# MoE layer of a hybrid block: when ScalarE copies gate outputs and gathered tokens, and behind which up tile TensorE folds the gate

## The reference

```python
def swiglu(h, wg, wu, wd):
    a = jnp.einsum('bsd,df->bsf', h, wg)
    b = jnp.einsum('bsd,df->bsf', h, wu)
    return jnp.einsum('bsf,fd->bsd', jax.nn.silu(a) * b, wd)

def moe_swiglu(h, router_w, wg, wu, wd):
    logits = jnp.einsum('bsd,de->bse', h, router_w).astype(jnp.float32)
    top_val, top_idx = lax.top_k(logits, TOP_K)
    gates = jax.nn.softmax(top_val, axis=-1)
    ...
    for e in range(N_EXPERTS):
        out = out + combine[..., e:e + 1].astype(h.dtype) * swiglu(h, wg[e], wu[e], wd[e])
```

## Time and profile before

| | us |
|---|---|
| median of 3 runs | 1413.13 |
| lowest and highest run | 1411.94, 1414.52 |
| profiled execution, its own time | 1415.2 |
| profiled execution, span of the core | 1413.4 |

### The profile page before, as it was taken

How to read it: one execution, slowest core, us unless ns; L and a number is a source line. 1 busy time by engine, 2 the same in 40 slices (tenths; PEclk the granted TensorE clock), 3 DMA queues, 4 the chain that set the end, 5 groups by cost and what they waited for, 6 DMA issues and landing times.

```text
span 1413.4 us, 17326 instructions
## 1 busy us (share of the span) xinstructions
PE 1364.1 (97%) x6732; PEld 1116.9 (79%) x6733; DVE 1143.1 (81%) x794; ACT 1001.7 (71%) x745; POOL 82.3 (6%) x72
## 2 busy tenths in 40 slices
PE   9999999999999999999999999999999999989996
PEld 7997788888799877877777878778777777767785
DVE  5886444544677688999989999988999997989997
ACT  6465434334556578788888888888888888878885
POOL 1011000000000021002000003000005000300000
PEclk9999999999999999999999999999999999999999
DMA  9637555655465349999999999999999999999993
GB/s 346 230 107 246 186 179 187 198 182 164 126 214 164 112 153 347 410 406 413 405 409 381 413 413 408 406 405 366 410 414 412 407 406 397 401 413 414 408 397 159
DMA packets 129530, 445.54 MB, mean 315 GB/s; under 512 B 9696, under 2 KB 13984, under 8 KB 114992
## 3 DMA queue, kind: packets, MB, share of 16 engines
q1 hardware_dynamic: 124912, 433.92, 80.5%
q0 software_dynamic: 2592, 7.45, 1.5%
q10 hardware_dynamic: 1952, 3.18, 0.6%
HBM read 437.70 MB, written 6.82 MB: 315 GB/s over the span
## 4 chain that ended last, share of the span: by engine, by line
PE 67%; DVE 14%; DMA 7%; issue 6%; ACT 5%; ACTq 0%; SPq 0%; DVEq 0%
PE ps L1588 18%; PE ps L1590 18%; PE ps L1589 18%; DVE w_lo L1407 10%; DMA raw<-in_moe_w_down_dram 4%; ACT w_hi L769 3%; DMA raw<-in_moe_w_gate_dram 2%; PE ps L1852 2%; PE ps L1854 2%; PE ps L1874 1%; DVE w_lo L1009 1%; PE ps L1880 1%; DMA raw<-in_moe_w_up_dram 1%; PE ps L1936 1%; ACT fold L818 1%
## 5 line engine op out<-in xcount | busy, mean ns | idle before, releaser
L1407 DVE TENSOR_TENSOR w_lo<-raw,w_hi 128x2048 fp32r<-128x2048 f32 x333 | 749.6, 2288 | 66.9 <-ACT w_hi L769 64.6
L769 ACT ACTIVATE w_hi<-raw 128x2048 fp32r<-128x2048 f32 x332 | 630.8, 1916 | 132.8 <-PE ps L1590 75.9
L1009 DVE TENSOR_TENSOR w_lo<-raw,w_hi 128x2048 fp32r<-128x2048 f32 (+2 forms) x81 | 176.8, 2186 | 98.6 <-ACT w_hi L587 98.3
L587 ACT ACTIVATE w_hi<-raw 128x2048 fp32r<-128x2048 f32 (+2 forms) x81 | 148.2, 1831 | 102.4 <-PE ps L1590 101.5
L1852 PE MATMUL ps<-w_hi,aG 128*128 128x512 f32 x448 | 183.9, 410 | 12.5 <-DVE w_lo L1407 11.7
L1854 PE MATMUL ps<-w_lo,aG 128*128 128x512 f32 x448 | 177.5, 396 | 0.0
L1588 PE MATMUL ps<-w_hi,aG 128*128 128x512 f32 x448 | 175.1, 391 | 2.4 <-DVE w_lo L1407 2.4
L1590 PE MATMUL ps<-w_hi,aG 128*128 128x512 f32 x448 | 174.5, 389 | 0.0
L1589 PE MATMUL ps<-w_lo,aG 128*128 128x512 f32 x448 | 174.4, 389 | 0.0
L1588 PE MATMUL ps<-w_hi,aT_hi 128*128 128x512 f32 (+2 forms) x432 | 161.0, 373 | 4.4 <-DVE aT_lo L1028 2.6
L1590 PE MATMUL ps<-w_hi,aT_lo 128*128 128x512 f32 (+2 forms) x432 | 158.2, 366 | 0.0
(11 more groups left out here) (341 smaller groups left out, 1762.0 us busy)
## 6 DMA issues: line engine op xcount, KB each, us to landing
raw<-in_moe_w_gate_dram SPq DMA_DIRECT2D x112, 1024.0 KB, 9.4
raw<-in_moe_w_up_dram SPq DMA_DIRECT2D x112, 1024.0 KB, 9.7
raw<-in_moe_w_down_dram SPq DMA_DIRECT2D x112, 1024.0 KB, 9.4
raw<-in_w_in_dram SPq DMA_DIRECT2D x20, 1024.0 KB, 6.9
raw<-in_ffn_w_gate_dram SPq DMA_DIRECT2D x14, 1024.0 KB, 5.1
raw<-in_ffn_w_up_dram SPq DMA_DIRECT2D x14, 1024.0 KB, 5.1
raw<-in_ffn_w_down_dram SPq DMA_DIRECT2D x14, 1024.0 KB, 5.0
raw<-in_w_out_dram SPq DMA_DIRECT2D x8, 1024.0 KB, 5.1
```

The source lines that it names most:

```text
L587: nc.scalar.activation(w_hi[:, slot % SPL, 0:n], raw[:, slot, 0:n], ACT.Copy).then_inc(hi_ready, 1)
L769: nc.scalar.activation(moe_hi(pos), raw[:, slot, :], ACT.Copy).then_inc(hi_ready, 1)
L1009: V.tensor_tensor(w_lo[:, slot % SPL, 0:n], raw[:, slot, 0:n], w_hi[:, slot % SPL, 0:n].bitcast(F32), ALU.subtract).then_inc(lo_ready[slot ...
L1407: V.tensor_tensor(moe_lo(pos), raw[:, pos % 6, :], moe_hi(pos).bitcast(F32), ALU.subtract)\
```

## The change

Three things move; no instruction is added or taken away.

1. On ScalarE `copy_g(7)` stands ahead of the split of tile 80 instead of behind it. This is so in all four pairs.
2. Where a next pair follows (three times), the copies of gather fills 0 and 1 stand ahead of `silu_b(7)` and `copy_u(7)` instead of behind them.
3. On TensorE the gate fold of the wide side-B units (1, 3 and 5) stands behind the second up tile instead of the first. In unit 7 it stays behind the first. This is twelve places in the four pairs.

```diff
@@ -851,14 +851,15 @@
                 silu(6, u0, g0)
                 splits(73, 77)
                 evac_sT(6, u0)
-                splits(78, 80)
+                splits(78, 79)
                 copy_g(7)
-                splits(81, 82)
+                splits(80, 82)
+                if more:
+                    gather_pair(p, 0)
+                    gather_pair(p, 1)
                 silu_b(7)
                 copy_u(7)
                 if more:
-                    gather_pair(p, 0)
-                    gather_pair(p, 1)
                     splits(83, 83)
                     gather_pair(p, 2)
                     gather_pair(p, 3)
@@ -1917,7 +1918,7 @@
                     pe.wait_ge(m_sT_lo, u0 + i)
                     for t in range(tiles):
                         proj(i, U_AT[i] + t, 2, t)
-                        if is_b(i) and t == 0:
+                        if is_b(i) and t == (1 if wide(i) else 0):
                             pe.wait_ge(g_copied, b0 + (i + 1) // 2)
                             fold_in(0, 0, 2 if wide(i) else 1, g_folded)
```

## The result

The changed kernel took 1415.86 us, the median of 20 runs, against 1413.53 us for 20 runs of the kernel before. The ratio is 1.0015, with a 95% interval of 1.0008 to 1.0022: slower, by 1.1 to 3.1 us, where 0.2 us less was forecast. The profiled execution took 1415.27 us, its span is 1413.4 us, and its mean granted clock is 0.992, against 1415.2, 1413.4 and 0.994 before.

The account below looks back on a forecast made before the run. The prediction took the weight stream to bound the kernel, each pair lasting as long as its loads. Clock 0.1 and last pair 0.1, all else 0, took 0.2 us off 1413.13, giving 1412.9 us, range 1410.2 to 1415.4.

Parts of the forecast that it names:

- used up, to within 0.1 us: Unit 3 of the first pair: the late gate fold ends at 616.1 to 616.2, SiLU starts at 616.11, leaving no slack.
- the named reason: Between pairs: gather copy 2 stays behind the split of tile 83, so fill 4 waits out the 1.2 us gained at fill 2.
- the clock: Second transition: the new waits might spare a 1.2 GHz stretch on TensorE that cost 0.3 us; counted as 0.1 us gained.
- The sum: Whole kernel: 0 for three transitions, 0.1 clock, 0 wide folds, 0.1 last pair, together 0.2 us less.
- are no longer than the 1.33 and 1.77 of before: Argument against a clock loss: TensorE's two new waits per transition, about 1.5 and 1.3 us, don't exceed the old ones.
- a loss of 1.7 us on TensorE cost 0.3 us: Second transition before the change: pairs of 220.2 and 220.5 us around a 1.2 GHz stretch price its lost work.
- slower by the clock: Rival: two TensorE waits bring each transition to 1.2 GHz, 3.4 us if all passes on, 1416.3 us; chance 0.06.
- a pair lasts as long as its loads: Full pairs: the weight stream runs all the time, 88.1 MB in 220 us, 400 GB/s.
- gaps of TensorE: Rival: TensorE's gaps count in full because loads follow it, 4.7 us less together, 1408.4 us; chance 0.09.
- The last pair: Last pair, no gather following: the split of tile 82 may start up to 0.1 us sooner; counted as 0.1 us gained.

Follow-up runs that it names:

- its repeat: The changed kernel with all three parts, run again unedited beside the kernel before: median 1414.83 us, 1.0009 times before.
- The kernel with gather copy 2 moved: Kernel before with gather copies 0 to 3 behind the splits of tiles 82 and 83, ahead of SiLU and up copy, up fold later: median 1412.32 us, 0.9994.
- Part 2 alone: Kernel before with only gather copies 0 and 1 moved ahead of SiLU and the up copy: median 1415.07 us, 1.0010 times before.
- the kernel with gathers and gate copy moved: Kernel before with gather copies behind splits of tiles 82 and 83, up fold later, gate copy one tile sooner: median 1412.98 us, 0.9994 times before.
- the four kernels with moved gathers: Kernel before with gather copies behind splits 82 and 83, up fold later; alone, plus part 1, parts 1 and 3, part 1 and zero matmuls: means 1412.42, 1412.62, 1413.27, 1412.22 us.
- the third-tile run: Kernel before with the gate fold of units 1, 3 and 5 behind the third up tile: median 1418.77 us, 1.0042 times before.

## Why the prediction was wrong

**Right: every move of a wait.** The gate copy's waits are gone; fill 2 comes 1.2 us sooner after tile 82's landing; a wait of 1.38 us, forecast at 1.2 to 1.4, stands ahead of fill 4; fill 4 itself stands where it stood, to 0.1 us. From one landing of tile 82 to the next it took 219.5 and 220.6 us, where 220 to 221 was forecast. At the tightest place of part 3 SiLU doesn't wait in the profiled execution of the changed kernel, and waits 0.4 us in that of its repeat, a little more than "used up, to within 0.1 us" allowed. The kernel with gather copy 2 moved shows that the named reason was the real one: with that copy sooner, the wait ahead of fill 4 is not there, and one of 0.9 us stands ahead of fill 6.

**Wrong: the clock, the step that failed.** The sum gave it a gain of 0.1 us and a rival of 0.06, where it turned out a loss of 0.9 to 1.3 us, for two reasons. The first was that the new waits "are no longer than the 1.33 and 1.77 of before". The second was the price: "a loss of 1.7 us on TensorE cost 0.3 us", read from one pair of 220.2 us before the stretch of the earlier trace rows and one of 220.5 behind it. The price was a sample of one. The pair of 220.2 us is the longest of the sixteen without a stretch; over all of them the price is 1.2 us, four times as much. And the waits were not only to be compared in length: the changed kernel's are no longer than those of before, and its clock is 0.0010 lower. Part 2 alone, with about as many waits and none longer, points the same way, by 0.0008 ± 0.0005. So the rival "slower by the clock" is the case that came, at 6 of 15 transitions instead of at none or at each. By 6 of 15 against 1 of 33 a transition has 0.37 stretches more, three transitions 1.1, and at 1.2 us each that is 1.3 us. The clock's own difference, 0.0010 at 0.9 us for each 0.001, gives 0.9 us. Of the 3.0 us between the forecast of 1412.9 and the measured 1415.86, another 0.4 is no effect of the change: the three runs of before had a median of 1413.13, the twenty beside the changed kernel 1413.53. The Trainium skill (TensorE: Matmul & The Clock Gate, A second HAM failure mode: psum-queue depth-cycling) says of another kernel that small idle times of TensorE between groups of matmuls, repeated often enough, cost throughput through the clock; the trace agrees in kind, with stretches at 0.50 behind waits of 1.4 to 2.6 us.

**Wrong by a little: "a pair lasts as long as its loads".** The share of 1.02 looked like a stream that can't go faster. Here are the windows of the first full pairs of the kernel with gathers and gate copy moved:

```profile
724.70:942.70 218.00, 212.55 (x943) 167.94 (x942) 201.86 (x102) 184.38 (x119) 11.25 (x7) 1.00 1.02 407
942.70:1161.60 218.90, 213.69 (x949) 168.87 (x949) 202.27 (x102) 184.68 (x119) 18.74 (x11) 1.00 1.02 408
```

The share is the same 1.02, and these pairs are 1.1 to 2 us shorter than the first two of the earlier trace rows. In the mean the eight such pairs of the four kernels with moved gathers take 218.7 us, 0.5 us less than the sixteen of 219.2 us. So gaps of TensorE seem to count in part: with fills 2 and 4 1.2 us sooner a pair is about 0.5 us shorter.

**Part 3**, counted at 0, with a cost between -0.3 and +0.1 us at each of two places, measures 0.5 ± 0.3 us. If it is not noise, it is more than the 0.25 us that SiLU's waits give by the slope of the third-tile run. Its share can't be settled with a scatter of 1 us from run to run.

**The last pair**, counted at +0.1, can't be read: from the third to the fourth landing of tile 82 the kernels scatter from 223.5 to 225.9 us.

**What stays open.** Why the stretch follows a transition in some executions and not in others, and why kernels with a wait ahead of fill 4 have it more often than those with one of the same length ahead of fill 2. And about 0.4 us of the 1.3 us of parts 1 and 2, which the clock's slope doesn't cover and which is no more than its error.

## What to carry to other kernels

Before moving an operation ahead in an in-order queue, follow the next one that the waiting engine needs: if that one stays where it is, the wait only moves, and a moved wait on TensorE can cost clock although no idle time was added. Price what a clock stretch costs from many stretches or many executions, not from one pair of stages. When a change is worth less than the scatter from run to run, compare the mean granted clock beside the time: it told parts 1 and 2 (clock down) from part 3 (clock unchanged), where the times of single kernels could not.

## What the runs showed that I had not expected

Work that computes nothing can raise the clock: five matmuls of zeros per transition, 1.3 us of TensorE's time where it stood idle, brought the mean granted clock of the kernel before from 0.9941 to 0.9955 and no loss in time (0.6 ± 0.4 us faster).

A stretch at 1.2 GHz can stand near the start of a launch, long before the code that was changed:

```profile
11.10:14.50 3.40, 3.16 (x12) 2.28 (x13) 3.40 (x5) 3.26 (x7) 2.62 (x5) 0.50 1.05 386
```

In the profiled execution of the changed kernel it is there, and its first weight load of the mixture is issued at 437.07 us, against 435.57 in that of before, which has none. That is 1.5 us which the change can't have caused through its own code. Twelve of the sixteen profiled executions have such a stretch, at 10 to 12 us or at 73 to 76 us, some of the fastest kernels among them, and the four without it all issue that load before 436 us. A single span compared with another carries this chance with it. Here the spans of before and after happened to be equal, 1413.4 us each, while the medians differ by 2.3 us; counted from that first load, the changed kernel's profiled execution is even 1.5 us the shorter one.
